# Depthwise convolution of a Conformer block: four channel tiles on each of two engines, and shifted copies placed by DMAs

## The chip, the cores and the metric

The kernel runs on one core of a Trainium2 chip, all in float32. The time is the device time of one execution in microseconds, the median over several runs. Of each kernel one more execution was recorded by the hardware profiler.

The core has engines with instruction streams of their own, which wait for each other by semaphores: TensorE (PE: matmuls and transposes into PSUM, which is used here as a ring of six banks of 512 columns and two fixed ones), VectorE (DVE), ScalarE (ACT), GpSimd (POOL) and SyncE (SP). SyncE issues nearly all DMAs here. Two hardware queues carry DMAs: q1 those of SyncE, q10 those of ScalarE; both are worked off by the same 16 DMA engines.

## The reference, cut to what matters

The program is a Conformer block followed by two attention/convolution layers with mixtures of experts. The change lies in the Conformer's convolution module, near the start. 512 tokens, 1024 channels, eight segments of 64 tokens:

```python
u = h @ w_pw1 + b_pw1                       # 1024 -> 2048
a, gate = jnp.split(u, 2, axis=-1)
u = a * jax.nn.sigmoid(gate)                # GLU
u = dwconv(u.reshape(B * n_seg, L // n_seg, D), w_dw).reshape(B, L, D) + b_dw   # 31 taps, each channel by itself
u = jax.nn.silu(layer_norm(u, ln_g, ln_b))
return u @ w_pw2 + b_pw2
```

The depthwise convolution is zero-padded within each segment: out[t] = sum over k of w[k] * u[t + k - 15].

## The kernel before

Channels lie on partitions, 128 to a tile, so there are eight channel tiles j = 0..7 of 128 x 512. For each tile:

- `pw1(j)` on TensorE: 16 matmuls (32 instructions in the profile) into two banks, one for the gate and one for the value. ScalarE evicts both (L925) into `glu_s` and `glu_a`, which have two buffers each, so `pw1(j)` on ScalarE waits until tile j-2 has been read.
- A tile of `PE_CONV` (0, 2, 4, 6, 7) is convolved on TensorE. The taps are grouped as 31 = 8 rounds of 4 shifts. `urep` (two buffers) holds for each group c of 32 channels the gated tile four times, on partitions 32r to 32r+31 shifted by r tokens; one matmul with a 128 x 32 weight tile then adds four taps for 32 channels, and 32 matmuls (64 instructions, L1540) make the tile. `glu(j)` on VectorE multiplies value and gate in 8 pieces of 32 x 512 straight into the places of r = 0 and 1 (L2309). `spread` on ScalarE copies to the places of r = 2 and 3 in 8 pieces (L933). GpSimd makes the tap weights `taps` (two buffers, L759). `conv_out` evicts with the bias (L940).
- A tile of `DVE_CONV` (1, 3, 5) is convolved on VectorE by `own_conv(j)`: the GLU into a padded buffer (L2316), then 31 multiply-adds of 128 x 512, each waiting for the one before (L2324, L2328).

`conv_mean(j)` (L1550) adds each finished tile to a mean over channels in a fixed bank; after the last one, `mean_done` lets ScalarE, then VectorE go on with the layer norm. `mod_gemv(1)` (L1489) is a matrix-vector product for later modulation parameters; `mod_turn(1)` (L1506) transposes its row.

The order on each engine is written out by hand. On TensorE `mod_gemv(1)` stands between conv(6) and conv(7). Two mean sums, conv(7), `mod_turn(1)` and the last two mean sums follow.

SyncE issues the weight loads in the order of a list, each as soon as the earlier owner of its slot in a six-slot ring is done (L531 to L541). The loads that matter here: one adaptation block of 2 MB (rows of 8 KB) each when pw1(1), pw1(3), pw1(5) and pw1(7) have ended; then two more such blocks and the two 2 MB blocks of w_pw2 (rows of 2 KB), all four released by the end of `mod_gemv(1)` (`mod_row` = 2). Behind the load for pw1(5) SyncE issues eight small loads (L646 to L650).

Of the kernel before, what the change touches and what calls it, by code (L numbers as in the profile page):

```python
# [12 lines left out]
P = 128  # L13
# [24 lines left out]
N_TAPS = 12  # L38
PE_CONV = (0, 2, 4, 6, 7)
DVE_CONV = (1, 3, 5)  # L40
# [19 lines left out]
for _n, _w in (  # L60
    ("c", 8), ("c2", 8), ("cctx", 8), ("norm1_g", 8), ("norm2_g", 8), ("final_g", 8), ("b_pw1", 16), ("b_dw", 8),
    ("ln_g", 8), ("ln_b", 8), ("b_pw2", 8), ("mix_g", 16), ("ffn_g", 16),
    ("b_mod0", 48), ("b_mod1", 48), ("w_conv3", 24), ("q_g", 1), ("k_g", 1), ("subln", 1), ("to_next_row", 5),
    ("b_mod2", 48), ("w_own0", TAPS), ("w_own1", TAPS), ("to_next_block", 18),
    ("w_dw", ROUNDS * 32), ("w_own2", TAPS),
):
    COL[_n] = _at
    _at += _w
VEC_ROWS = [128, 123, 48 + 2 * TAPS, 128, 128, TAPS]
# [47 lines left out]
def block_kernel(nc, A, out):  # L117
# [31 lines left out]
    for j in range(DT):  # L149
        T_PW1[j] = tiles(["act"] * 2)  # L150
        if j == 0:
            T_TAPS = tiles(["dve"])
        if j % 2:
# [102 lines left out]
    with ExitStack() as ctx:  # L256
# [18 lines left out]
        vecT = sb("vecT", [P, 5 * P + TAPS])  # L275
# [75 lines left out]
        glu_s = carve(arena, 11264, 2, N)  # L351
        hid = carve(arena, 0, 16, N)
# [70 lines left out]
        for name in (  # L423
# [6 lines left out]
            "u_base", "u_ready", "u_spread", "u_own", "conv_done", "mean_done", "mean_sb", "centered",  # L430
            "x_pw2", "gains", "hid_ready", "mlp_wsum", "mlp_wsum4", "mlp_tsum", "mlp_part", "mlp_m1", "mlp_read",
            "x_mlp", "rope_tab", "f_folded", "feature_w", "x_sq", "x_sq_used", "x_ms", "x_ms_sb", "x_rms", "x_inv", "x_wide", "x_scaled", "c_ms", "c_rms", "c_inv", "ctx_scaled", "ctx_ready", "lam_sum", "lam_exp",
            "in_hsum", "in_wsum", "in_part", "in_m1", "in_read", "qk_raw", "qk_sq", "qk_ms", "qk_root", "qk_inv", "qk_scaled", "qk_turn", "qk_roped", "qk_turned", "qk_done",
            "scores", "score_half", "neg_max", "probs", "attn_ready", "attn_turned", "aT_sb", "pv_done", "o_in", "o_eps", "o_ms",
            "o_rms", "o_inv", "o_scaled", "o_turned", "o_ready",
            "router_gain", "affine_in", "router_shift", "logit_parts", "logit_parts_sb", "shift_sb", "logits_ready", "soft_exp", "aff_ready", "pos_ready", "left_ready", "left_turned", "chosen",
# [93 lines left out]
        def _(sp):  # L530
# [100 lines left out]
            def load_taps():  # L631
# [6 lines left out]
                for m, j in enumerate(DVE_CONV):  # L638
                    dst = vec_rows[0:TAPS, 5, :] if m == 2 else vec_rows[48 + TAPS * m:48 + TAPS * (m + 1), 2, :]
# [44 lines left out]
        def _(pool):  # L684
# [67 lines left out]
            for m, j in enumerate(PE_CONV):  # L752
                if m >= 2:
                    pool.wait_ge(S["tile_done"], T_CV[PE_CONV[m - 2]] + 1)
                elif m == 0:
                    pool.wait_ge(*emptied(T_TAPS)(0))
# [64 lines left out]
        def _(act):  # L821
# [511 lines left out]
        def _(pe):  # L1333
# [197 lines left out]
            def conv(j):  # L1531
# [4 lines left out]
                pe.wait_ge(S["u_ready"], m + 1)  # L1536
                pe.wait_ge(S["u_spread"], m + 1)
# [7 lines left out]
            def conv_mean(j):  # L1545
# [664 lines left out]
        def _(dve):  # L2210
# [85 lines left out]
            def glu(j):  # L2296

                m = PE_CONV.index(j)
                u = urep[m % 2]
                dve.wait_ge(*emptied(T_PW1[j])(1))  # L2300
                if m >= 2:
                    dve.wait_ge(S["tile_done"], T_CV[PE_CONV[m - 2]] + 1)
                elif m == 0:
                    dve.wait_ge(S["pads_zero"], 5)
                for r in (0, 1):
                    for c in range(SHIFTS):
                        a, s = (x[32 * c:32 * c + 32, j % 2, :].rearrange("p (s w) -> p s w", s=SEGS)
                                for x in (glu_a, glu_s))
                        ins = dve.tensor_tensor(u[32 * r:32 * r + 32, c, :, PAD - r:PAD - r + SEG], a, s, ALU.mult)  # L2309
                    ins.then_inc(S["u_ready" if r else "u_base"], 1)  # L2310

            def own_conv(j):

                m = DVE_CONV.index(j)
                dve.wait_ge(*emptied(T_PW1[j])(1))
# [4 lines left out]
                for k in range(TAPS):  # L2320
# [6 lines left out]
                    else:  # L2327
                        ins = dve.scalar_tensor_tensor(out=acc, in0=u, scalar=w, in1=acc, op0=ALU.mult, op1=ALU.add)  # L2328
# [738 lines left out]
```

## Time and profile before

| | us |
|---|---|
| median of 3 runs | 2239.44 (2238.3 to 2242.77) |
| profiled execution | 2237.22 |
| its span | 2235.4 |
| PE busy | 2165.0 (97%) |
| DVE busy | 967.1 (43%) |
| ACT busy | 396.1 (18%) |
| POOL busy | 73.0 (3%) |

The profile covers the span from the first to the last instruction. Its page gives for each engine busy time and share; the chain that ended last is 83% PE, 11% DMA, 3% DVE and 1% ACT. TensorE's clock was granted at 0.987 of full speed on the mean. The Conformer's convolution stage lies between about 37 and 198 us. Answers of the trace for single stretches (timelines, packets per DMA queue, windows) are used besides the page; all their times count from the span's start.

### The profile page before, as it was taken

The page shows a single profiled execution, that of the slowest core. Times are in us where ns is not written, and L with a number is a line of the kernel's source. Part 1 is how long each engine was busy: PE and PEld are TensorE (multiplying, and loading weights), DVE is VectorE, ACT ScalarE, POOL GpSimd, SP SyncE. Part 2 cuts the span into 40 slices and gives each one's busy share as a digit, 9 for nine tenths or more (in the row PEclk, how much of TensorE's full clock was granted, in tenths as well). Part 3 has the DMA queues.
Part 4 walks back from the last instruction along what each step waited for, and adds up shares of the span by engine and source line. Part 5 has one row for each costly group of instructions (what it writes and reads, how often), then busy time and mean ns, then how long its engine had stood idle before and what let it go on. Part 6 is the DMA issues. An engine that isn't in the chain of part 4 may idle for free.

```text
span 2235.4 us, 24839 instructions
## 1 busy us (share of the span) xinstructions
PE 2165.0 (97%) x10126; PEld 1289.8 (58%) x10126; DVE 967.1 (43%) x1403; ACT 396.1 (18%) x781; POOL 73.0 (3%) x92
## 2 busy tenths in 40 slices
PE   7999999999999999998999999999999899999998
PEld 3343488888886777855444444437884544444443
DVE  3883297787855544833112222215551322222222
ACT  3214222002113122842100000002000200000000
POOL 1100100000012000000000000001001000000000
PEclk9999999999999999998999999999999899999999
DMA  9316234567650112032899999997111599999996
GB/s 353 155 44 234 105 137 164 205 247 271 219 207 22 54 45 83 1 151 113 355 429 429 428 429 428 428 414 264 38 76 75 228 425 428 428 429 429 428 429 269
DMA packets 106459, 564.23 MB, mean 252 GB/s; under 512 B 8840, under 2 KB 17550, under 8 KB 78734
## 3 DMA queue, kind: packets, MB, share of 16 engines
q1 hardware_dynamic: 105952, 563.03, 62.6%
q8 instruction: 54, 0.88, 0.2%
q14 instruction: 23, 0.19, 0.0%
q10 hardware_dynamic: 430, 0.13, 0.0%
HBM read 561.04 MB, written 2.10 MB: 252 GB/s over the span
## 4 chain that ended last, share of the span: by engine, by line
PE 83%; DMA 11%; DVE 3%; ACT 1%; issue 1%; DVEq 0%; SPq 0%; POOL 0%; ACTq 0%
PE psum L1593 20%; PE psum L2036 16%; PE psum L1347 10%; PE psum L2022 8%; DMA ring<-in_moe_w_down_dram 6%; PE psum L2115 5%; PE psum L1741 4%; PE psum L2072 3%; PE psum L1765 3%; PE psum L1922 2%; DMA ring<-in_mlp_w_dram 2%; PE psum L1898 2%; PE psum L1873 2%; DMA ring<-in_moe_w_up_dram 2%; PE psum L1540 2%; PE psum L1489 1%
## 5 line engine op out<-in xcount | busy, mean ns | idle before, releaser
L2036 PE MATMUL psum<-ring,arena 128*64 128x512 f32 x2048 | 444.6, 593 | 5.1 <-DMA ring<-in_moe_w_up_dram 5.1
L2036 PEld LDWEIGHTS psum<-ring,arena 128*64 128x64 f32 x2048 | 145.0, 137 | 301.4 <-issue 287.0
L2022 PE MATMUL psum<-ring,arena 128*64 128x512 f32 x768 | 224.5, 594 | 2.1 <-DMA ring<-in_moe_w_down_dram 2.1
L2884 DVE TENSOR_TENSOR arena<-psum,arena 128x512 f32<-128x512 f32 x32 | 33.9, 1059 | 410.1 <-PE psum L2036 410.1
L1347 PE MATMUL psum<-hT,ring 128*128 128x512 f32 x416 | 180.6, 593 | 3.0 <-ACT hT L888 3.0
L1593 PE MATMUL psum<-ring 128*128 128x256 f32 x640 | 142.9, 380 | 3.8 <-DVE rstd L2467 3.8
L1593 PE MATMUL psum<-hT,ring 128*128 128x256 f32 x608 | 138.9, 385 | 0.8 <-ACT hT L882 0.8
L1347 PEld LDWEIGHTS psum<-hT,ring 128*128 128x128 f32 x416 | 78.6, 190 | 101.6 <-issue 96.9
L1593 PEld LDWEIGHTS psum<-ring 128*128 128x128 f32 x640 | 121.0, 190 | 23.6 <-issue 7.5
L2072 PEld LDWEIGHTS psum<-arena 128*128 128x128 f32 x1024 | 119.7, 196 | 14.0 <-issue 14.0
L1593 PEld LDWEIGHTS psum<-hT,ring 128*128 128x128 f32 x608 | 117.1, 193 | 18.4 <-issue 2.2
L2072 PE MATMUL psum<-arena 128*128 128x128 f32 x1024 | 123.9, 281 | 2.5 <-DVE arena L2911 2.5
L2022 PEld LDWEIGHTS psum<-ring,arena 128*64 128x64 f32 x768 | 73.5, 137 | 73.5 <-issue 73.5
L2022 PE MATMUL psum<-hT,arena 128*64 128x512 f32 x256 | 113.2, 595 | 1.7 <-issue 1.7
L2115 PE MATMUL psum<-arena 128*128 128x512 f32 x256 | 114.1, 599 | 0.0
L2903 DVE SCALAR_TENSOR_TENSOR xT<-psum,modv,xT 128x512 f32<-128x512 f32 x128 | 96.1, 751 | 17.8 <-PE psum L2115 5.8
L1593 PE MATMUL psum<-arena,ring 128*128 128x256 f32 x448 | 99.8, 380 | 3.0 <-DMA ring<-in_mlp_w_dram 3.0
L2898 DVE COPY arena<-psum 128x512 f32<-128x512 f32 x16 | 11.1, 692 | 204.7 <-PE psum L2022 204.7
L1593 PEld LDWEIGHTS psum<-arena,ring 128*128 128x128 f32 x448 | 84.4, 190 | 17.8 <-DMA ring<-in_mlp_w_dram 4.2
L2115 PEld LDWEIGHTS psum<-arena 128*128 128x128 f32 x256 | 47.3, 190 | 66.6 <-issue 66.6
L1275 ACT ACTIVATE arena<-psum 128x512 f32<-128x512 f32 x32 | 19.1, 597 | 327.7 <-PE psum L2036 327.7
L2328 DVE SCALAR_TENSOR_TENSOR arena<-arena,vecT 128x512 f32<-128x512 f32 x90 | 72.3, 803 | 3.2
(384 smaller groups left out, 2555.9 us busy)
## 6 DMA issues: line engine op xcount, KB each, us to landing
ring<-in_moe_w_gate_dram SPq DMA_DIRECT2D x64, 2048.0 KB, 19.2
ring<-in_moe_w_up_dram SPq DMA_DIRECT2D x64, 2048.0 KB, 16.2
ring<-in_moe_w_down_dram SPq DMA_DIRECT2D x44, 2048.0 KB, 19.8
ring<-in_ada_w_dram SPq DMA_DIRECT2D x24, 2048.0 KB, 8.6
ring<-in_mlp_w_dram SPq DMA_DIRECT2D x16, 2048.0 KB, 8.6
hT<-in_moe_w_down_dram SPq DMA_DIRECT2D x16, 2048.0 KB, 14.5
ring<-in_w_mod_dram SPq DMA_DIRECT2D x12, 2048.0 KB, 12.7
ring<-in_conv_w_in_dram SPq DMA_DIRECT2D x6, 2048.0 KB, 19.4
```

The source lines that it names most:

```text
L1347: ins = pe.matmul(bank[:, 0:width], w[:, k, col:col + P], src(k), start=start and k == 0, stop=stop and k == kts - 1)
L1540: ins = pe.matmul(bank[32 * c:32 * c + 32, :, :], taps[m % 2][:, g, c, :], u[:, c, :, SHIFTS * g:SHIFTS * g + SEG], start=g == 0, stop=g = ...
L1593: ins = pe.matmul(psum[:, t % 6, H * i:H * i + H], w[:, k, P * i:P * i + P], src[:, k, :], start=first and i == 0 and k == 0, stop=True, s ...
L1741: ins = pe.matmul(psum[:, t % 6, at:at + width], src[:, k, :], w[:, k, :], start=first and k == 0, stop=k == DT - 1, skip_group_check=True)
L1765: ins = pe.matmul(psum[:, t % 6, H * i:H * i + H], hs[:, k, P * i:P * i + P], ws[:, k, :], start=first and i == 0 and k == 0, stop=True, s ...
L1873: ins = pe.matmul(psum[:, banks + bank, at:at + hi - lo], qT[64 * c:64 * c + 64, h, m * P:(m + 1) * P], kT[64 * c:64 * c + 64, h, lo:hi], ...
L2022: ins = pe.matmul(psum[64 * e:64 * e + 64, bank + nh, :], src[:, 4 * h + k, 64 * e:64 * e + 64], w[:, k, nh * N:(nh + 1) * N], start=h == ...
L2036: ins = pe.matmul(psum[64 * nh:64 * nh + 64, bank + e, :], src[:, 4 * h + k, 64 * e:64 * e + 64], w[:, k, nh * N:(nh + 1) * N], start=h == ...
L2072: ins = pe.matmul(psum[:, 6 + half, (fj % 4) * P:(fj % 4 + 1) * P], h_tok[:, tt, fj * P:(fj + 1) * P], hot[:, tt, :, :].rearrange("p a b - ...
L2115: pe.matmul(psum[:, SCATTER[fj % 3], :], y_sb[:, fj * P:(fj + 1) * P], gselT, start=True, stop=True)\
L2328: ins = dve.scalar_tensor_tensor(out=acc, in0=u, scalar=w, in1=acc, op0=ALU.mult, op1=ALU.add)
L2903: dve.scalar_tensor_tensor(out=xT[:, fj, :], in0=psum[:, SCATTER[fj % 3], :], scalar=modv[:, 1 + 2 * layer, 40 + fj:41 + fj], in1=xT[:, fj ...
```

## The change

TensorE now convolves tiles 2, 4, 6, 7, and VectorE 0, 1, 3, 5. VectorE's own tiles need one more set of tap weights, hence one more small load by SyncE and a second transposed tile of taps. `glu(j)` for a TensorE tile is one multiplication of 128 x 512 into `rms` or `rstd`, buffers that are free in this stage. `spread(m)` on ScalarE no longer copies: it issues 16 DMAs, one for each r and c, each moving 32 partitions x 8 segments of 64 numbers (256 B) from there into `urep`. TensorE waits for their semaphore, `u_spread0` or `u_spread1`. The order on TensorE, ScalarE and VectorE is new.

```diff
@@ -35,9 +35,10 @@
 H = N // 2
 EPS = 1e-6
 N_VEC = 21
-N_TAPS = 12
-PE_CONV = (0, 2, 4, 6, 7)
-DVE_CONV = (1, 3, 5)
+N_TAPS = 13
+PE_CONV = (2, 4, 6, 7)
+DVE_CONV = (0, 1, 3, 5)
+MEANS = (0, 2, 1, 4, 3, 6, 5, 7)
 UPAD = SEG + TAPS - 1
 LAM_INIT = 0.2
 RING = 6
...
@@ -349,6 +350,7 @@
         upad = carve(arena, 2 * UREP + (DT - 1) * N, SEGS, UPAD)
         glu_a = carve(arena, 10240, 2, N)
         glu_s = carve(arena, 11264, 2, N)
+        glu_out = [rms[:, :], rstd[:, :]]
...
@@ -926,13 +929,16 @@
                                    bias=vecT[:, col:col + 1]).then_inc(FREE["act"], 1)
 
             def spread(m):
+
                 u = urep[m % 2]
-                act.wait_ge(S["u_base"], m + 1)
-                for r in (2, 3):
+                act.wait_ge(S["u_ready"], m + 1)
+                if m >= 2:
+                    act.wait_ge(S["tile_done"], T_CV[PE_CONV[m - 2]] + 1)
+                for r in range(SHIFTS):
                     for c in range(SHIFTS):
-                        ins = act.activation(u[32 * r:32 * r + 32, c, :, PAD - r:PAD - r + SEG],
-                                             u[0:32, c, :, PAD:PAD + SEG], ACT.Copy)
-                ins.then_inc(S["u_spread"], 1)
+                        act.dma_start(u[32 * r:32 * r + 32, c, :, PAD - r:PAD - r + SEG],
+                                      glu_out[m % 2][32 * c:32 * c + 32, :].rearrange("p (s w) -> p s w", s=SEGS))\
+                            .then_inc(S[f"u_spread{m % 2}"], 16)
 
             def conv_out(j):
                 t = T_CV[j]
@@ -940,14 +946,16 @@
                 act.activation(cv[:, j, :], psum[:, t % 6, :], ACT.Identity,
                                bias=vecT[:, COL["b_dw"] + j:COL["b_dw"] + j + 1]).then_inc(FREE["act"], 1)
 
-            for m in range(4):
-                pw1(2 * m)
+            pw1(0)
+            pw1(1)
+            for m in range(3):
+                pw1(2 * m + 2)
                 spread(m)
-                pw1(2 * m + 1)
-                conv_out(2 * m)
-                if m == 3:
-                    spread(4)
-            mod_row(1)
+                pw1(2 * m + 3)
+                if m == 2:
+                    spread(3)
+                    mod_row(1)
+                conv_out(2 * m + 2)
             act.wait_ge(S["conv_done"], len(DVE_CONV))
             conv_out(DT - 1)
             mod_turned(1)
...
@@ -1533,8 +1541,7 @@
                 u = urep[m % 2]
                 bank = begin(t).rearrange("p (s w) -> p s w", s=SEGS)
                 pe.wait_ge(S["taps_ready"], m + 1)
-                pe.wait_ge(S["u_ready"], m + 1)
-                pe.wait_ge(S["u_spread"], m + 1)
+                pe.wait_ge(S[f"u_spread{m % 2}"], 16 * SHIFTS * SHIFTS * (m // 2 + 1))
...
-                return pe.matmul(psum[:, STAT, :], const("ones_d"), cv[:, j, :], start=j == 0, stop=j == DT - 1)
-
-            for m in range(4):
-                pw1(2 * m)
-                if m == 0:
-                    pe.wait_ge(S["taps_in"], 16 * N_TAPS)
-                    pe.wait_ge(S["tap_pad"], 1)
-                    turn_tile(T_TAPS, [(vec_rows[0:VEC_ROWS[g], g, :], VEC_ROWS[g]) for g in range(2, 6)])
-                if m == 2:
-                    pe.wait_ge(S["rms_ready"], 1)
-                if m >= 2:
-                    conv_mean(2 * m - 3)
-                pw1(2 * m + 1)
-                conv(2 * m)
-                if m == 3:
-                    mod_gemv(1)
-                if m:
-                    conv_mean(2 * m - 2)
-            conv_mean(5)
+                return pe.matmul(psum[:, STAT, :], const("ones_d"), cv[:, j, :], start=j == MEANS[0], stop=j == MEANS[-1])
+
+            pw1(0)
+            pe.wait_ge(S["taps_in"], 16 * N_TAPS)
+            pe.wait_ge(S["tap_pad"], 1)
+            for m in range(2):
+                turn_tile(T_TAPS + m, [(vec_rows[0:VEC_ROWS[g], g, :], VEC_ROWS[g]) for g in (2 + 2 * m, 3 + 2 * m)])
+            pw1(1)
+            pw1(2)
+            pw1(3)
+            conv(2)
+            pw1(4)
+            pe.wait_ge(S["rms_ready"], 1)
+            conv_mean(0)
+            conv_mean(2)
+            pw1(5)
+            conv(4)
+            pw1(6)
+            conv_mean(1)
+            conv_mean(4)
+            pw1(7)
+            conv_mean(3)
+            mod_gemv(1)
+            conv(6)
             conv(7)
             mod_turn(1)
             conv_mean(6)
+            conv_mean(5)
             conv_mean(7).then_inc(S["mean_done"], 1)
...
@@ -2296,22 +2309,16 @@
             def glu(j):
 
                 m = PE_CONV.index(j)
-                u = urep[m % 2]
                 dve.wait_ge(*emptied(T_PW1[j])(1))
                 if m >= 2:
-                    dve.wait_ge(S["tile_done"], T_CV[PE_CONV[m - 2]] + 1)
-                elif m == 0:
-                    dve.wait_ge(S["pads_zero"], 5)
-                for r in (0, 1):
-                    for c in range(SHIFTS):
-                        a, s = (x[32 * c:32 * c + 32, j % 2, :].rearrange("p (s w) -> p s w", s=SEGS)
-                                for x in (glu_a, glu_s))
-                        ins = dve.tensor_tensor(u[32 * r:32 * r + 32, c, :, PAD - r:PAD - r + SEG], a, s, ALU.mult)
-                    ins.then_inc(S["u_ready" if r else "u_base"], 1)
-
-            def own_conv(j):
+                    dve.wait_ge(S[f"u_spread{m % 2}"], 16 * SHIFTS * SHIFTS * (m // 2))
+                dve.tensor_tensor(glu_out[m % 2], glu_a[:, j % 2, :], glu_s[:, j % 2, :], ALU.mult).then_inc(S["u_ready"], 1)
+
+            def own_conv(j, between=None):
 
                 m = DVE_CONV.index(j)
+                if m:
...
+                        if between is not None and k == TAPS // 2:
+                            glu(between)
...
-            for j in range(DT):
-                if j in PE_CONV:
-                    glu(j)
-                else:
-                    own_conv(j)
+            dve.wait_ge(S["pads_zero"], 5)
+            own_conv(0)
+            glu(2)
+            own_conv(1)
+            glu(4)
+            own_conv(3)
+            own_conv(5, 6)
+            glu(7)
```

TensorE around its last two convolutions. Before: L1540 is a convolution (`tmp` or `sq` hold the tap weights), L1489 `mod_gemv(1)`, L1550 a mean sum.

```order
L1540 MATMUL psum<-arena,tmp 32x512 [waits u_ready,u_spread,taps_ready,act_free]
L1540 MATMUL psum<-arena,tmp 32x512 x31
L1489 MATMUL psum<-ring,cpad 32x512 [waits landed2,mod_raw_ready]
L1489 MATMUL psum<-ring,cpad 32x512 x7
...
L1550 MATMUL psum<-arena,K 128x512 [waits act_free]
L1550 MATMUL psum<-arena,K 128x512 [waits conv_done]
L1540 MATMUL psum<-arena,sq 32x512 [waits u_ready,u_spread,taps_ready,act_free]
L1540 MATMUL psum<-arena,sq 32x512 x31
L1506 MATMUL psum<-K,mod_rows 128x128 [waits mod_row_sb]
```

The same place now; L1547 is a convolution, L1497 `mod_gemv(1)`, L1557 a mean sum.

```order
L1557 MATMUL psum<-arena,K 128x512 [waits conv_done]
L1497 MATMUL psum<-ring,cpad 32x512 [waits landed2,mod_raw_ready]
L1497 MATMUL psum<-ring,cpad 32x512 x7
...
L1547 MATMUL psum<-arena,sq 32x512 [waits u_spread0,taps_ready,act_free]
L1547 MATMUL psum<-arena,sq 32x512 x31
L1547 MATMUL psum<-arena,tmp 32x512 [waits u_spread1,taps_ready,act_free]
L1547 MATMUL psum<-arena,tmp 32x512 x31
L1514 MATMUL psum<-K,mod_rows 128x128 [waits mod_row_sb]
```

`mod_gemv(1)` has moved ahead of conv(6), and conv(7) follows conv(6) at once.

VectorE at the end of the stage, before: a GLU in eight pieces (L2309), the last own convolution (L2316 to L2328, tile 5), and the GLUs of tiles 6 and 7.

```order
L2309 TENSOR_TENSOR arena<-arena 32x8x64 [waits tile_done,act_free]
L2309 TENSOR_TENSOR arena<-arena 32x8x64 x7
L2316 TENSOR_TENSOR arena<-arena 128x8x64 [waits act_free]
L2324 TENSOR_SCALAR arena<-arena,vecT 128x512 [waits dve_link]
L2328 SCALAR_TENSOR_TENSOR arena<-arena,vecT 128x512 [waits u_own]
L2328 SCALAR_TENSOR_TENSOR arena<-arena,vecT 128x512 [waits dve_link] x29
L2309 TENSOR_TENSOR arena<-arena 32x8x64 [waits tile_done,act_free]
L2309 TENSOR_TENSOR arena<-arena 32x8x64 x7
L2309 TENSOR_TENSOR arena<-arena 32x8x64 [waits tile_done,act_free]
L2309 TENSOR_TENSOR arena<-arena 32x8x64 x7
```

The same now: tile 5 (L2323 to L2337) with the GLU of tile 6 (L2315, into `rms`) in its middle, and the GLU of tile 7 behind it.

```order
L2323 TENSOR_TENSOR arena<-arena 128x8x64 [waits act_free,conv_done]
L2331 TENSOR_SCALAR arena<-arena,vecT 128x512 [waits dve_link]
L2337 SCALAR_TENSOR_TENSOR arena<-arena,vecT 128x512 [waits u_own]
L2337 SCALAR_TENSOR_TENSOR arena<-arena,vecT 128x512 [waits dve_link] x13
L2315 TENSOR_TENSOR rms<-arena 128x512 [waits u_spread0,act_free,dve_link]
L2337 SCALAR_TENSOR_TENSOR arena<-arena,vecT 128x512
L2337 SCALAR_TENSOR_TENSOR arena<-arena,vecT 128x512 [waits dve_link] x15
L2315 TENSOR_TENSOR rstd<-arena 128x512 [waits u_spread1,act_free]
```

The eight-piece GLUs have become single instructions, and that of tile 6 stands after 14 of the 30 multiply-adds of tile 5.

ScalarE's new spreads, with the evictions of pw1 (L928) and the convolutions (L946) about the last two.

```order
L939 DMA arena<-rms 32x8x64 [waits tile_done,u_ready]
L939 DMA arena<-rms 32x8x64 x15
L928 ACTIVATE arena<-psum,vecT 128x512 [waits u_own,tile_done] x2
L939 DMA arena<-rstd 32x8x64 [waits tile_done,u_ready]
L939 DMA arena<-rstd 32x8x64 x15
L895 ACTIVATE mod_rows<-psum 128x512 [waits mod_row]
L946 ACTIVATE arena<-psum,vecT 128x512 [waits tile_done]
L946 ACTIVATE arena<-psum,vecT 128x512 [waits tile_done,conv_done]
```

Sixteen DMA issues stand where eight copies stood; the row of `mod_gemv(1)` (L895) is now evicted behind the last spread.

## Rows read from the trace of the kernel before

**Rows 1.** Chain that ended last: start us, us, what; 37 to 374 us.
```profile
37.33 13.97 PE psum L1347 x32
...
65.72 7.00 PE psum L1540 x64
...
100.39 7.00 PE psum L1540 x64
...
173.16 7.00 PE psum L1540 x64
180.16 6.87 PE psum L1489 x64
...
195.95 0.59 PE psum L1506 x4
196.53 1.73 PE psum L1550 x4
...
373.06 8.32 DMA ring<-in_mlp_w_dram
```

**Rows 2.** Timeline of DVE, 45 to 200 us: start, us, line, operation, idle before.
```profile
53.51 8.56 DVE L2309 TENSOR_TENSOR arena<-arena 32x512 f32<-32x512 f32 x8
...
66.48 0.69 DVE L2316 TENSOR_TENSOR arena<-arena 128x512 f32<-128x512 f32 x1 [4.40 <-ACT arena L925]
...
92.82 5.56 DVE L2309 TENSOR_TENSOR arena<-arena 32x512 f32<-32x512 f32 x8
...
198.92 1.29 DVE L2350 TENSOR_TENSOR arena<-arena,tmp 128x512 f32<-128x512 f32 x2 [19.43 <-ACT tmp L956]
```

**Rows 3.** Timeline of ACT, 0 to 60 us; ACTq are its DMA issues.
```profile
3.97 0.33 ACTq L525 DMA_DIRECT2D arena<-in_conv_ln_b_dram  x1
...
6.33 0.48 ACTq L525 DMA_DIRECT2D arena<-in_b_mod_dram  x1
...
51.34 0.69 ACT L925 ACTIVATE arena<-psum,vecT 128x512 f32<-128x512 f32 x1 [6.18 <-PE psum L1347]
```

**Rows 4.** Timeline of SP, 50 to 420 us: DMA issues.
```profile
137.21 0.47 SPq L646 DMA_DIRECT2D lam_in<-in_lam_q_dram  x1
...
141.30 2.27 SPq L650 DMA_DIRECT2D rw<-in_router_w_dram  x2
...
173.19 14.78 SPq L541 DMA_DIRECT2D ring<-in_w_mod_dram  x3
```

**Rows 5.** DMA packets in 100.3 to 101.3, 101.8 to 107.2, 203 to 207 us.
```profile
DMA packets 0, 0.00 MB, mean 0 GB/s; under 512 B 0, under 2 KB 0, under 8 KB 0
...
DMA packets 250, 1.99 MB, mean 369 GB/s; under 512 B 7, under 2 KB 7, under 8 KB 7
...
DMA packets 772, 1.55 MB, mean 387 GB/s; under 512 B 16, under 2 KB 16, under 8 KB 772
```

**Rows 6.** DMA packets by queue in 36 to 37 and in 143 to 152 us.
```profile
DMA packets 937, 0.17 MB, mean 167 GB/s; under 512 B 907, under 2 KB 923, under 8 KB 937
...
q1 hardware_dynamic: 937, 0.17, 92.3%
...
q1 hardware_dynamic: 2990, 0.57, 31.8%
```

**Rows 7.** DMA packets by queue in 11 to 12 us; q10 is ACT's.
```profile
DMA packets 94, 0.40 MB, mean 403 GB/s; under 512 B 12, under 2 KB 47, under 8 KB 47
...
q1 hardware_dynamic: 47, 0.39, 97.0%
q10 hardware_dynamic: 47, 0.02, 7.7%
```

**Rows 8.** Windows: us, engines' busy time, PEclk, DMA share, GB/s.
```profile
277.00:281.00 4.00, 3.79 (x9) 3.10 (x10) 3.77 (x8) 3.26 (x9) 0.00 (x0) 0.50 0.19 69
281.00:285.00 4.00, 4.00 (x19) 3.50 (x19) 4.00 (x10) 3.38 (x8) 0.00 (x0) 0.99 0.00 0
198.00:200.40 2.40, 0.25 (x1) 0.01 (x1) 1.48 (x3) 1.35 (x3) 0.00 (x0) 1.00 0.99 388
```

More of the change, by code:

```diff
@@ L64 @@
     ("b_mod2", 48), ("w_own0", TAPS), ("w_own1", TAPS), ("to_next_block", 18),
-    ("w_dw", ROUNDS * 32), ("w_own2", TAPS),
+    ("w_dw", ROUNDS * 32), ("w_own2", TAPS), ("w_own3", TAPS),
 ):
@@ L68 @@
     _at += _w
-VEC_ROWS = [128, 123, 48 + 2 * TAPS, 128, 128, TAPS]
+VEC_ROWS = [128, 123, 48 + 2 * TAPS, 128, 128, 2 * TAPS]
 KCOL = {}
@@ L151, in block_kernel @@
         if j == 0:
-            T_TAPS = tiles(["dve"])
-        if j % 2:
+            T_TAPS = tiles(["dve"] * 2)
+        if j % 2 and j > 1:
             T_CV[j - 1] = tiles(["act"])
@@ L274, in block_kernel @@
         K = sb("K", [P, KW])
-        vecT = sb("vecT", [P, 5 * P + TAPS])
+        vecT = sb("vecT", [P, 5 * P + 2 * TAPS])
         cpad = sb("cpad", [P, DT, 32])
@@ L429, in block_kernel @@
             "n_ms", "n_inv", "n_wide", "half_scaled", "half_ready", "late_sq",
[L430 removed]
+            "u_ready", "u_spread0", "u_spread1", "u_own", "conv_done", "mean_done", "mean_sb", "centered",
             "x_pw2", "gains", "hid_ready", "mlp_wsum", "mlp_wsum4", "mlp_tsum", "mlp_part", "mlp_m1", "mlp_read",
[L432 to L433 removed]
+            "x_mlp", "rope_tab", "f_folded", "feature_w", "x_sq", "x_sq_used", "x_ms", "x_ms_sb", "x_rms", "x_inv", "x_wide", "x_scaled", "c_ms", "c_rms", "c_inv", "ctx_scaled", "lam_sum", "lam_exp",
+            "in_hsum", "in_wsum", "in_part", "in_m1", "in_read", "qk_raw", "qk_sq", "qk_ms", "qk_root", "qk_inv", "qk_roped", "qk_turned", "qk_done",
             "scores", "score_half", "neg_max", "probs", "attn_ready", "attn_turned", "aT_sb", "pv_done", "o_in", "o_eps", "o_ms",
             "o_rms", "o_inv", "o_scaled", "o_turned", "o_ready",
[L436 removed]
+            "router_gain", "affine_in", "router_shift", "logit_parts", "logit_parts_sb", "shift_sb", "logits_ready", "soft_exp", "aff_ready", "left_ready", "left_turned", "chosen",
             "hot_ready", "gsel_ready", "gathered", "xs_act", "xs_dve", "gselT_done", "gselT_sb",
@@ L638, in load_taps @@
                 for m, j in enumerate(DVE_CONV):
-                    dst = vec_rows[0:TAPS, 5, :] if m == 2 else vec_rows[48 + TAPS * m:48 + TAPS * (m + 1), 2, :]
+                    at, g = (48 + TAPS * m, 2) if m < 2 else (TAPS * (m - 2), 5)
+                    dst = vec_rows[at:at + TAPS, g, :]
                     rows(sp, dst, A["conv_w_dw"][0][:, j * P:(j + 1) * P], "taps_in")
@@ L755, in _ @@
                 elif m == 0:
-                    pool.wait_ge(*emptied(T_TAPS)(0))
+                    pool.wait_ge(*emptied(T_TAPS)(1))
                     pool.wait_ge(S["sq_used"], DT)
@@ L2331, in own_conv @@
                 ins.then_inc(S["conv_done"], 1)
-            dve.wait_ge(S["tile_done"], T_TAPS + 1)
             for g in range(2, 6):
-                w = VEC_ROWS[g]
-                ins = dve.tensor_copy(vecT[:, g * P:g * P + w], psum[:, T_TAPS % 6, (g - 2) * P:(g - 2) * P + w])
-                if g < 5:
+                w, t = VEC_ROWS[g], T_TAPS + g // 2 - 1
+                dve.wait_ge(S["tile_done"], t + 1)
+                ins = dve.tensor_copy(vecT[:, g * P:g * P + w], psum[:, t % 6, g % 2 * P:g % 2 * P + w])
+                if g % 2:
+                    ins.then_inc(FREE["dve"], 1)
+                else:
                     link(ins)
-            ins.then_inc(FREE["dve"], 1)
-            dve.wait_ge(*emptied(T_TAPS)(0))
+            dve.wait_ge(*emptied(T_TAPS)(1))
             link(dve.memset(upad[:, :, 0:PAD], 0.0))
             link(dve.memset(upad[:, :, PAD + SEG:UPAD], 0.0))
-            for j in range(DT):
-                if j in PE_CONV:
-                    glu(j)
-                else:
-                    own_conv(j)
+            dve.wait_ge(S["pads_zero"], 5)
[6 more added lines that the diff above has]
+            glu(7)
             dve.wait_ge(S["mean_sb"], 1)
```

1 line of the change is left out of this document (added).

## The prediction

> **What bounds the kernel now.** I read the chain of waits first. From 37.33 us to 196.53 + 1.73 = 198.3 us it holds nothing but TensorE: eight first pointwise layers pw1 (L1347, 13.7 to 14.0 us for 32 matmul instructions), five convolutions (L1540, 7.00 us each), the mean sums (L1550), the adaptation product mod_gemv(1) (L1489, 6.87 us) and small transposes [rows 1]. So in this stage TensorE's own work is the time: a convolution taken from it is worth up to 7.00 us, and anything that makes it wait costs its full length. VectorE's timeline comes second. It ends its last GLU near 179 us and then stands idle for 19.43 us until the means are there [rows 2], so it has room for one more convolution. Third comes the traffic: which transfers SyncE's queue issues at what time [rows 4], and how the 16 DMA engines share themselves between two queues [rows 5 to 7].
>
> **What leaves TensorE.** conv(0) goes: −7.00 us [rows 1]. The four tap transposes become two tiles of two with the same work, and the eight means stay eight. From the same rows I shift the points that matter. pw1(3) ends at 100.39 − 7.00 = 93.4. pw1(7) ends at 173.16 − 7.00 = 166.2. mod_gemv(1) now stands ahead of conv(6), with five means before it for four: it ends at 180.16 + 6.87 − 14.00 + 0.87 = 173.9. conv(6) and conv(7) would then run from 173.9 to 187.9, and with mod_turn (0.59) and three means (3 × 0.87) the stage would end at 191.2 for 198.3 before: −7.1 us, if TensorE never waits.
>
> **What VectorE gets.** One own convolution lasts from 66.48 to 92.82, 26.34 us [rows 2]. The GLU for a TensorE tile falls from eight pieces (5.56 us) to one whole multiplication, for which I take the 0.69 us of L2316. Its dates: own_conv(0) starts where glu(0) did, 53.5 to 79.9. glu(2) needs pw1(2), done at 79.5 and evicted in 0.69 [rows 3]: ready at 81.0. own_conv(1) 81.0 to 107.4. glu(4) waits for pw1(4), done at 93.4 + 7.00 + 13.7 = 114.1: VectorE stands 7 us, and the GLU is ready at 115.6. own_conv(3) to 142.0. own_conv(5) with glu(6) in its middle (ready at 155.7) to 169.1. glu(7) ready at 169.9. The last sum is not late for its mean; what matters is that glu(7) is ready at 169.9 and conv(7) wants its data at 180.9.
>
> **What the placing costs.** ScalarE loses eight copies per tile (4.44 us) and issues 16 DMAs of 32 partitions × 8 pieces of 256 B: 4096 packets, 256 for each of the 16 engines. No row shows a DMA from SBUF to SBUF. Issue: ScalarE's take 0.33 to 0.48 us, SyncE's 128-packet ones 0.47, the 1024-packet ones 1.13 on average [rows 3, 4]. I take 0.47, by the nearest in packets, so 16 × 0.47 = 7.5 us; the ends are 0.33 (5.3 us) and 1.13 (18 us). Movement with nothing beside it: 937 mostly short packets moved in 1 us at 92.3% busy, 15.8 ns of one engine for each [rows 6], so 256 take 4.0 us and hide behind the issue. From issue to first packet a big load takes over 1 us (the one released by pw1(3)'s end at 100.3 has no packet to 101.3 and flows from 101.8) [rows 1, 5]; I use 1.3 for both queues and let 2 us stand for issue to semaphore.
> With that the first three are covered: spread(0) 81.0 + 7.5 + 2 = 90.5 for a need at 93.4; spread(1) 125.1 for 129.7 (pw1(5)'s end); spread(2) 165.2 for 173.9. While ScalarE issues, pw1's evictions wait up to 7.5 us; TensorE has six banks and doesn't notice.
>
> **The fourth meets the weight loads.** SyncE is held by mod_gemv(1): when it ends, SyncE issues the two remaining adaptation blocks and the two pw2 blocks, 8 MB in a row. Before, that was at 180.16 + 6.87 = 187.03, and the spreads were no transfers; now it is at 173.9 [rows 1, 4]. spread(3) issues from 169.9 to 177.4. By 173.9 it has 4.0 / 0.47 = 8.5 of its 16 DMAs out; the load of slot 1 (issued at 166.2, packets to about 173.0) has left the engines just before, and by 175.2, when the 8 MB arrive, these 8.5 are moved. 7.5 DMAs remain: 120 packets per engine.
> How do two queues share an engine? Between 11 and 12 us ScalarE's queue (q10) had short rows waiting beside adaptation loads on q1: 47 packets of the one went through and 47 of the other, and the engines were full [rows 7]. These were loads with three rows and a semaphore write per engine (35 rows and 12 under 512 B), so each short packet waited for one 8 KB packet, not each DMA. In the Trainium skill, DMA: Bandwidth & Descriptors, section Queues, rings and completion order, the engine goes round robin between its queues, packet by packet; by that rule, the trace agrees (47 to 47), but its further statement is a rival below.
> A pair takes 16 / 47 = 0.34 us on one engine. The two adaptation blocks are 256 packets each [rows 5], together 32 per engine: 32 × 0.34 = 10.9 us. The pw2 blocks come in 2 KB packets, 772 in 4 us or 0.083 us each [rows 5]; with a short one 0.099: the other 88 take 8.7 us. So spread(3) has landed at 175.2 + 19.6 + 0.2 = 195.0, and conv(7), wanted at 180.9, waits 14.1 us. Nothing stands before it on TensorE that could be done meanwhile: mod_turn and the last means are queued behind it.
> Then the clock. After the wide gap near 271 to 276 us the granted clock stood at 0.50 (1.2 GHz) from 277 to 281, with 9 matmuls where the next 4 us at 0.99 held 19: ten times 0.21 us, 2.1 us lost. After the 2.4 us gap at 198 it stayed 1.00 [rows 8]. A wait of 14 us is of the first kind: +2.1 us (bounds 0 and 7.0, all of conv(7) at 1.2 GHz).
> Sum: −7.1 + 14.1 + 2.1 = +9.1 us. Behind the stage TensorE's work and the loads that it releases follow each other (a load at 373.06 begins as TensorE gives its slot back [rows 1]), so I carry the shift to the end unchanged. Profiled execution: 2237.22 + 9.1 = 2246.3. The median of the runs shown lies 2.2 above it: 2248.5 us.
>
> **Rivals.**
> *Everything lands in time (20%).* If several of the short packets pass in one turn, spread(3) keeps ahead of conv(7). From nine on: 120 / 9 = 13 turns of 0.32 and 120 × 0.0158 us, 6.1 us, so 181.3, a wait of 0.4; from ten on, none. Then −7.1 us stands: 2232.4. For it: the rows that met the loads were loads from HBM with at most four packets per engine and DMA, these have 17. Against it: the even count, which held even with four. The Trainium skill, same page and section, has this as a rule: a whole packet of typically 9 to 17 descriptors is drained before the engine switches; by it the time would be about 2232. The count of rows 7 shows single ones.
> *Issue is quick, the meeting short (10%).* At 0.33 us per issue, 12 of 16 DMAs are out by 173.9, and 64 packets per engine remain: 32 × 0.34 + 32 × 0.099 = 14.1 us, landed at 189.4, a wait of 8.5. −7.1 + 8.5 + 2.1 = +3.5: 2243, not to be told from no change.
> *Every spread is slow (10%).* The six 128-packet loads and two of 1024 issued from 137 us on moved 2990 packets in the 9 us from 143 us on at 31.8% busy, up to 1.1 us per DMA [rows 4, 6]: if a small DMA costs this, or issue costs 1.13, a spread takes about 16 to 18 us and 2 to land. spread(0) lands near 99, and its end falls into the load issued at 93.4, so 101: a wait of 7.6. spread(1) lands some 4 to 7 us late, spread(3) at about 198. With three fallen clocks: −7.1 + 7.6 + 5.5 + 17 + 5 = +28: 2267. Against it: at 36 us seven such DMAs' worth of packets passed in 1 us [rows 6].
>
> **How the numbers follow.** The forecast has 60%; its own range, from the bounds of issue (0.40 to 0.6 us) and clock (0 to 4 us), is 2243 to 2254. The 80% range must hold the hidden case too and leaves most of the slow-spread one out: 2231 to 2259. A measurement tells 0.2%, about 4.5 us, from no change. Faster is the hidden case and little else: 0.21. Within 0.2%: the short meeting and the low end of the forecast, 0.10. Slower: 0.69.
>
> **What the profile of the changed kernel would show.** Right: one wait of TensorE of 12 to 16 us ahead of the last convolution, ended by a DMA; packets of q10 and q1 in equal number from about 175 us; clock near 0.5 behind it; no wait ahead of the first three convolutions; VectorE idle 7 us ahead of glu(4). Wrong: conv(7) following conv(6) at once; q10 packets many times those of q1; issues of 1 us on ScalarE; or a later stage that gives the shift back.

## The result

The changed kernel is slower: 2256.74 us median of 5 runs (2252.23 to 2259.08) for 2241.83 of the kernel before in the same measurement (5 runs, 2238.3 to 2242.77). The ratio is 1.0066, 95% interval 1.0053 to 1.0079. A second measurement gave 2257.95 for 2241.8, ratio 1.0071 (1.0054 to 1.0087). The forecast was 2248.5, +9.1 us; it is +14.9 and +16.2. That lies inside the 80% range (2231 to 2259) and above the range that the forecast gave for itself (2243 to 2254).

The profiled execution took 2254.87 us (span 2253.1), 17.65 more than the one before. The chain that ended last, through the stage of the change; it answers to [rows 1]. Columns: start us, us, what.

```profile
37.64 16.54 PE psum L1355 x32
...
94.39 2.17 DMA arena<-rms
...
96.70 7.07 PE psum L1547 x64
...
178.47 1.72 ACTq L939
...
182.22 3.77 ACTq L939
...
186.01 16.73 DMA arena<-rstd
...
202.88 8.92 PE psum L1547 x64
211.80 0.59 PE psum L1514 x4
212.39 2.59 PE psum L1557 x6
```

The place to read is 186.01: the last of the DMAs that place tile 7 is issued there and lands 16.73 us later; conv(7) starts at 202.88, and its 64 instructions take 8.92 us for 7.00. In the waits of TensorE between 37 and 300 us (total, times, longest) the two of the convolutions are

```profile
PE psum L1547 <- DMA arena<-rstd: 18.6, 1, 18.6
...
PE psum L1547 <- DMA arena<-rms: 0.6, 1, 0.6
```

conv(7) waits 18.6 us, conv(2) 0.6, conv(4) and conv(6) not at all. ScalarE's timeline has the spreads, 16 DMA issues each:

```profile
84.38 10.65 ACTq L939 DMA_DIRECT2D arena<-rms  x16
...
158.57 10.52 ACTq L939 DMA_DIRECT2D arena<-rms  x16
...
171.65 18.29 ACTq L939 DMA_DIRECT2D arena<-rstd  x16
```

An undisturbed spread is issued in 10.5 to 10.65 us, about 0.63 us and a gap of 0.03 for each DMA, and the last DMA lands 2.2 us after its own issue began. The fourth took 18.29 us to issue: three single issues, at 178.47, 182.22 and 186.01 us, took 1.72, 3.77 and 3.93 us. VectorE and SyncE's queue, answering to [rows 2] and [rows 4]:

```profile
118.46 0.69 DVE L2315 TENSOR_TENSOR rstd<-arena 128x512 f32<-128x512 f32 x1 [7.78 <-ACT arena L928]
...
170.93 0.68 DVE L2315 TENSOR_TENSOR rstd<-arena 128x512 f32<-128x512 f32 x1
```

```profile
169.57 9.00 SPq L543 DMA_DIRECT2D ring<-in_w_mod_dram  x3
178.61 10.60 SPq L543 DMA_DIRECT2D ring<-in_conv_w_pw_dram  x2
```

VectorE stands 7.78 us ahead of glu(4), and glu(7) starts at 170.93. SyncE issues the block released by pw1(7) at 169.57, the next two when mod_gemv(1) has ended at 177.2, and the pw2 blocks from 178.61. Packets per queue (packets, MB, share of 16 engines) in 178 to 180, 188 to 190 and 196 to 198 us, answering to [rows 7]:

```profile
q10 hardware_dynamic: 1042, 0.25, 116.3%
q1 hardware_dynamic: 14, 0.11, 27.7%
...
q1 hardware_dynamic: 96, 0.79, 98.1%
q10 hardware_dynamic: 96, 0.02, 5.5%
...
q1 hardware_dynamic: 299, 0.59, 89.6%
q10 hardware_dynamic: 302, 0.07, 17.6%
```

From 178 to 180 the spread has the engines nearly alone. Later each queue moves one packet for one of the other: 96 beside 96 of 8 KB, 302 beside 299 of 2 KB. From 180 us to the end q10 moved 1959 packets, 122 for each engine (semaphore writes counted).

There are two stretches in which the queues don't take turns. From 172 to 175 us the block released by pw1(7) flows; the spread, issued from 171.65 on, moves nothing at all, so q10 has no row. From 180 to 183 us the 8 MB have just begun:

```profile
q1 hardware_dynamic: 153, 1.25, 100.4%
...
q1 hardware_dynamic: 131, 1.07, 93.9%
q10 hardware_dynamic: 64, 0.02, 4.3%
```

The queue wasn't empty: by 180.2 us 11 DMAs of 17 packets per engine were issued, 2992 packets, and up to 180 us 2393 had moved, so about 37 per engine were waiting. In both stretches a load that has begun shortly before flows on q1 while packets issued on q10 wait. No run shows why.

The clock (PEclk is the third last column), answering to [rows 8]:

```profile
38.00:42.00 4.00, 4.00 (x5) 1.46 (x5) 3.31 (x6) 4.00 (x7) 0.00 (x0) 0.50 0.79 247
...
190.00:202.80 12.80, 0.00 (x0) 0.00 (x0) 0.00 (x0) 1.16 (x2) 0.00 (x0) 0.50 1.06 342
...
202.80:206.00 3.20, 3.12 (x16) 0.90 (x20) 0.00 (x0) 0.00 (x0) 0.00 (x0) 0.50 0.44 161
...
206.00:212.00 6.00, 6.00 (x54) 1.84 (x47) 0.00 (x0) 0.08 (x1) 0.00 (x0) 0.95 0.00 0
```

PEclk fell to 0.50 (1.2 GHz) in the long wait and stayed there to about 206 us. It also stood at 0.50 from 38 to 42 us, in the first pw1, which took 16.54 us for 13.97.

So the 17.65 us are: 0.3 us by which the stage began later; 2.6 in the first pw1 (clock); −7.0 for conv(0); 0.6 ahead of conv(2); 18.6 ahead of conv(7); 1.9 in conv(7) (clock). That makes 17.0, in a stage whose end moved by 16.7; the 0.3 between them were not traced. mean_done came at 214.98 for 196.53 + 1.73 = 198.26 in the kernel before [rows 1], and the shift stayed to the end.

### The profile page after: what moved, and what is told of

It is laid out like the page before. It is cut to its first block, busy times and chain, and to the rows that moved or that the text cites. A ratio compares the mean times of both kernels' runs of the same rounds, so it can differ in the third digit from the quotient of the medians.

```text
span 2253.1 us, 24730 instructions
## 1 busy us (share of the span) xinstructions
PE 2165.2 (96%) x10062; PEld 1292.8 (57%) x10062; DVE 964.7 (43%) x1399; ACT 373.3 (17%) x740; POOL 70.7 (3%) x91
## 4 chain that ended last, share of the span: by engine, by line
PE 62%; issue 23%; DMA 7%; DVE 6%; ACTq 1%; ACT 1%; POOL 0%; DVEq 0%; SPq 0%; POOLq 0%
PE psum L1606 21%; PE psum L2049 8%; PE psum L1355 7%; PE psum L2035 4%; PE psum L1754 4%; PE psum L1778 3%; DMA ring<-in_moe_w_down_dram 3%; DVE arena L2337 3%; PE psum L2128 3%; PE psum L1935 2%; PE psum L2085 2%; PE psum L1911 2%; PE psum L1886 2%; DMA ring<-in_mlp_w_dram 1%; ACTq L939 1%
## 5 line engine op out<-in xcount | busy, mean ns | idle before, releaser
L2337 DVE SCALAR_TENSOR_TENSOR arena<-arena,vecT 128x512 f32<-128x512 f32 x120 | 93.3, 777 | 4.2
## 6 DMA issues: line engine op xcount, KB each, us to landing
ring<-in_moe_w_up_dram SPq DMA_DIRECT2D x64, 2048.0 KB, 16.2
ring<-in_w_mod_dram SPq DMA_DIRECT2D x12, 2048.0 KB, 13.7
```

## The experiments

My theory after this, called the turns theory: conv(7)'s wait is the meeting of the spread of tile 7 with 8 MB of weight loads, and its length comes from packets taking turns. The rivals: the DMAs are slow by themselves; the spread comes behind all of the loads; the loss is elsewhere. "Before" in the times of the first four is 2243.75 us, the median of 14 runs (2239.05 to 2247.38).

**Loads held until the spread has landed (e1_hold).**

```diff
                 if prev_of[n] is not None:
...
+                if n == B_MOD[2][2]:
+                    sp.wait_ge(S["u_spread1"], 2 * 16 * SHIFTS * SHIFTS)
```

> The changed kernel, but SyncE issues the two adaptation blocks and the two pw2 blocks (8 MB) only when the spread of tile 7 has landed. Turns theory (the 18.6 us wait ahead of conv(7) comes from sharing the 16 DMA engines packet by packet with these loads): spread(3) takes 10.5 us of issue and 2.2 to land, as spread(0) did, so about 183.5 us in the trace of the changed kernel, and conv(7) waits 0 to 2 us for 18.6; no fallen clock there; the whole is 17 to 20 us faster than the changed kernel, about 2237 to 2240. The loads end near 206 us and are wanted at about 200 (first half) and 210, so they cost nothing. Rival (the DMAs are slow by themselves: sixteen issues behind a busy ScalarE): conv(7) still waits over 8 us. Rival (most of the loss is elsewhere, such as the 2.6 us at the stage's start): the gain stays under 10 us.

Measured: 2233.28 us (2232.0 to 2235.82, 5 runs), ratio to before 0.9954 (0.9941 to 0.9968). TensorE's wait for tile 7, and ScalarE's issue of it:

```profile
PE psum L1549 <- DMA arena<-rstd: 1.3, 1, 1.3
```

```profile
171.88 12.22 ACTq L941 DMA_DIRECT2D arena<-rstd  x16
```

One wait in SyncE's program takes 23.5 us from the changed kernel's time. TensorE's wait is 1.3 us for 18.6, and the last spread is issued in 12.22 us for 18.29. So the issues of 3.77 and 3.93 us belong to the meeting. That of 1.72 us doesn't: with the loads held, one issue still takes 1.59 us at the same place, 179.19. The rivals "slow by themselves" and "elsewhere" fall. The time lies below the 2237 to 2240 expected, of which more below.

**mod_gemv(1) back between the two convolutions (e2_between).**

```diff
-            mod_gemv(1)
             conv(6)
+            mod_gemv(1)
             conv(7)
```

> The changed kernel with mod_gemv(1) between conv(6) and conv(7), as before the change: same work, other order, and the 8 MB are released 7 us later. Turns theory: spread(3) has left the engines when they come; conv(6), wanted at about 170.5, now waits some 1 to 3 us for spread(2), conv(7) not at all or under 2 us; 15 to 19 us faster than the changed kernel, about 2238 to 2242. Rival (slow by themselves): the wait only moves to conv(6) and conv(7), over 8 us in sum.

Measured: 2233.03 us (2230.94 to 2235.78, 4 runs), ratio 0.9953 (0.9938 to 0.9969). The waits of the convolutions:

```profile
PE psum L1547 <- DMA arena<-rms: 1.0, 2, 0.6
...
PE psum L1547 <- DMA arena<-rstd: 0.2, 1, 0.2
```

With the same work in another order conv(7) waits 0.2 us. The waits for the other buffer are 0.6 us ahead of conv(2) and 0.4 ahead of conv(6), less than the 1 to 3 expected, and the time lies below the 2238 to 2242 expected. What costs isn't the transfers by themselves but the loads released beside them.

**The same bytes in smaller packets (e3_two_kb).**

```diff
...
+                elif n in B_MOD[2][2:]:
+                    for q in range(4):
+                        sp.dma_start(slot_like(slot, src)[:, :, q * N:(q + 1) * N], src[:, :, q * N:(q + 1) * N])\
+                            .then_inc(landed[slot], 16)
```

> The changed kernel, but each of the two adaptation blocks that meet the spread is loaded by four DMAs of a quarter of the columns: the same bytes in packets of 2 KB for 8 KB. Turns theory (one packet of each queue in turn): a turn of the spread costs 0.1 us for 0.34, so the packets left, some 100 to 115 per engine, take about 11 us for 18 to 20; conv(7)'s wait falls from 18.6 to 9 to 12 us, though all bytes are the same. Rival (the engines share by bytes, or the spread simply comes behind the loads): the wait stays at 17 to 20 us. In time 7 to 10 us faster than the changed kernel, or no change.

Measured: 2249.34 us (2247.53 to 2251.19, 9 runs), ratio to before 1.0026 (1.0016 to 1.0036), 7.4 us faster than the changed kernel's first median. TensorE's wait, and the queues from 188 to 190 us:

```profile
PE psum L1551 <- DMA arena<-rstd: 13.7, 1, 13.7
```

```profile
q1 hardware_dynamic: 302, 0.58, 89.4%
q10 hardware_dynamic: 304, 0.07, 18.0%
```

The wait fell by 4.9 us to 13.7, and 9 to 12 was expected, so that number missed; the rival, no change, is ruled out. The 7.4 us in time lie within the 7 to 10 expected, but the stage's end came only 4.3 us earlier (210.6 for 215.0), so part of them isn't the wait and stays unexplained. The counts say why the wait was longer than expected: from 180 us on the spread had 2210 packets left, 138 per engine, where I had taken 100 to 115. At 302 to 304 packets in 2 us a turn takes 0.105 us, and 138 turns 14.5 us; the spread landed at 197.66, about 17.7 us after 180, with a slow stretch from 182 to 184 (63 packets, beside 345 of q1) like that of the changed kernel. What decides is the number of turns left and what stands in each.

**Copies on ScalarE for the DMAs (e4_copies).**

```diff
-                        act.dma_start(u[32 * r:32 * r + 32, c, :, PAD - r:PAD - r + SEG],
-                                      glu_out[m % 2][32 * c:32 * c + 32, :].rearrange("p (s w) -> p s w", s=SEGS))\
-                            .then_inc(S[f"u_spread{m % 2}"], 16)
+                        ins = act.activation(u[32 * r:32 * r + 32, c, :, PAD - r:PAD - r + SEG],
+                                             glu_out[m % 2][32 * c:32 * c + 32, :].rearrange("p (s w) -> p s w", s=SEGS),
+                                             ACT.Copy)
+                ins.then_inc(S[f"u_spread{m % 2}"], 1)
...
```

> The changed kernel with the DMAs of spread replaced by sixteen copies of 32 x 512 on ScalarE, from the same gated tile to the same places: 16 x 0.555 = 8.9 us by the copies of the kernel before. It tells what the split of tiles (four and four) brings without the transfers. Theory: the split is worth its 7 us when the placing is hidden: spread(3) is ready about 180.5 in the changed kernel's trace, before conv(7) wants it; no wait of TensorE for ScalarE above 1 us; about 7 us faster than the kernel before, 2232 to 2237. Rival (ScalarE is blocked 8.9 us per tile and evicts pw1 late, or VectorE with four own convolutions is the bound): waits of TensorE for evictions or means of several us, and no gain over the kernel before.

Measured: 2232.6 us (2228.55 to 2234.3, 5 runs), ratio 0.9953 (0.9939 to 0.9966): faster than both kernels. ScalarE's last spread:

```profile
169.68 10.30 ACT L939 ACTIVATE arena<-rstd 32x512 f32<-32x512 f32 x16 [1.40 <-DVE rstd L2316]
```

From one copy to the next it was 0.64 us, not 0.555, so a spread takes 10.3 us; it is ready at 180.0, and conv(7) starts at 182.1, when conv(6) is done. None of the convolutions waits. The split of four and four is sound; ScalarE places a tile itself in no more time than it needs to issue the DMAs for it.

**Half the segments (e5_half_seg).** Each DMA places segments 0 to 3 only, so half of the shifted copies is missing.

```diff
-                        act.dma_start(u[32 * r:32 * r + 32, c, :, PAD - r:PAD - r + SEG],
+                        act.dma_start(u[32 * r:32 * r + 32, c, 0:SEGS // 2, PAD - r:PAD - r + SEG],
...
```

> The changed kernel, but each DMA of spread places only the first four of eight segments (128 packets for 256; the other half of the shifted copies is left out). An issue took 0.63 us on ScalarE where I had 0.47. If an issue costs by its packets, it falls to about 0.45 us and a spread to 7.5 us; if it costs by the DMA, it stays at 0.6 us and the spread at 10.5 us. Turns theory: when the 8 MB come at about 180, half of the 122 packets per engine are left, 61: 30 of them beside 8 KB packets, 31 beside 2 KB, 10.2 + 3.3 us, so conv(7) waits 9 to 12 us for 18.6. Rival (the spread comes behind the loads whatever its size): the wait stays above 16 us.

Measured: 2244.2 us in one run, before 2241.8 (7 runs). Wait, an undisturbed spread's issue, and the queues from 184 to 186 us:

```profile
PE psum L1548 <- DMA arena<-rstd: 10.6, 1, 10.6
```

```profile
155.54 10.39 ACTq L939 DMA_DIRECT2D arena<-rms  x16
```

```profile
q1 hardware_dynamic: 96, 0.79, 98.6%
q10 hardware_dynamic: 96, 0.02, 5.6%
```

128 packets are issued in the 0.65 us of 256: the issue costs by the DMA. The wait is 10.6 us, within the 9 to 12 that the turns gave, and the queues are even again. A spread that came behind all of the loads would have waited over 16. For a time it does come behind them, though: from 177 to 179 us, with 18 packets per engine or more issued and not moved, q10 has no row in the view, and q1 is alone:

```profile
q1 hardware_dynamic: 101, 0.83, 102.6%
```

And from 175.93 us on, beside these loads, no issue takes over 0.72 us, so loads on the other queue are not enough to make an issue slow.

**Where does the clock at the stage's start come from? (e6_before_again, e7_after_again: both kernels unchanged.)**

> The kernel before once more, for a second profile. Its profiled execution (2237.2 us) was the shortest of all its runs (median 2243.8 of 14). If the missing 3 to 6 us are the clock at the start of the stage, the first pw1 takes about 16.5 us here for 13.97, with the granted clock near 0.5 from 38 to 42 us, as in the profiles of the changed kernel and of the first four experiments; then the gain of 10 to 11 us in the timed runs of the hidden versions is not larger than their 7 us by the change. If the first pw1 takes 14 us again, the kernel before loses its time elsewhere.

> The changed kernel once more. Turns theory: again a wait of 17 to 20 us ahead of conv(7) and about 2 us of half clock behind it; 13 to 17 us slower than the kernel before on this chip. If the wait differs by several us from run to run, the meeting with the loads depends on chance.

The kernel before took 2241.79 us in this execution. Its first pw1, and its window from 38 to 42 us:

```profile
36.77 15.70 PE psum L1347 x32
```

```profile
38.00:42.00 4.00, 4.00 (x7) 1.59 (x6) 2.12 (x4) 3.98 (x6) 0.00 (x0) 0.69 0.89 274
```

15.70 us for 13.97, with the clock at 0.69: the slow first pw1 is the kernel before's too, and its first profile was a lucky one. The changed kernel again took 2257.95 us (2256.21 to 2259.45, 4 runs), with

```profile
PE psum L1547 <- DMA arena<-rstd: 20.5, 1, 20.5
```

```profile
203.51 9.29 PE psum L1547 x64
```

20.5 us of wait for 18.6, just over the 17 to 20 expected, and 9.29 us of conv(7): the meeting is there both times, and its size moves by 2 us. Single issues took 4.43 and 4.18 us here.

**More profiles (e8_before_c, e9_before_d: the kernel before; e10_copies_again; e11_hold_again).** The held and copied versions gained 10 to 11 us, more than conv(0)'s 7.

> The kernel before, third profile. The versions with the spread hidden are 10 to 11 us faster in the timed runs, but their stage (start to mean_done) is only 3.4 (held loads) to 7.1 us (copies) shorter than in the kernel before's second profile. Theory A: the feed-forward part behind the stage (from the first L1593 to the first L1741 matmul: 416.6 and 418.3 us in the two profiles before, 414.1 to 417.3 in seven of the changed kind) is longer in the kernel before by some 2 us, and more in its slower runs. Then this profile shows 417 or more there. Theory B: it is scatter of the clock anywhere; then this part lies within 415 to 417 and the missing microseconds appear at another place or not at all.

> The kernel before, fourth profile; expectation as for the third. If its whole time is above 2243, the stretch that is long against the first profile (2237.2 us) tells where the slower runs lose.

> The copies version, second profile. Theory A: 414 to 416 us from the first L1607 to the first L1755 matmul (the same two places); the stage ends at 191 to 194 us. Theory B: that part can be 417 or more here too.

> The held-loads version, second profile. Turns theory: conv(7) waits 1 to 2 us again and the stage ends at 194 to 197 us. Theory A: about 415 us in the feed-forward part; theory B: anywhere in 414 to 418.

From each profile I took the start of the token sums behind pw2 (L1374 in the kernel before) and the length of the feed-forward part as the expectation defines it. All in us; "run" is the time of the profiled execution.

| kernel | run | token sums start | feed-forward part |
|---|---|---|---|
| before | 2237.2, 2241.8, 2241.4, 2243.1 | 270.1, 271.2, 274.9, 273.0 | 416.6, 418.3, 415.3, 417.2 |
| changed | 2254.9, about 2256.2 | 286.8, 289.5 | 417.3, 416.0 |
| held loads | 2235.1, 2233.6 | 267.9, 266.6 | 415.3, 414.7 |
| copies | 2228.6, 2231.6 | 264.1, 264.2 | 414.1, 415.4 |
| mod_gemv(1) between | 2233.0 | 266.6 | 415.8 |

(The second run of the changed kernel is its span, 2254.4, and 1.8.) By the means, the copies version is at the token sums 272.3 − 264.15 = 8.1 us ahead of the kernel before, and gains another 2.1 in the feed-forward part. At the end of the stage itself (the last mean sum) the kernel before is at 198.3, 199.4, 201.4 and 199.7 us and the copies version at 192.3 and 192.4: 7.3 us apart, which is what conv(0) was said to be worth. Both copies and held loads ended the stage where expected (192.4 and 194.8 us in the second profiles), and conv(7) waited 1.3 us again with the loads held. Theory A, "417 or more in each profile before", falls with 415.3; "some 2 us on the mean" stands on four profiles against two and is within their scatter. The first pw1 explains none of it on the mean: it took 13.97 to 16.57 us in the kernel before, 15.5 on the mean, and 15.5 in both profiles of the copies. The step from 7.3 to 8.1 us is the clock behind the stage: from the last mean sum to the token sums it is 72 us in two profiles before and in both of the copies, and 1.5 to 1.7 us more in the third and fourth before, where the clock stood at 0.57 on the mean from 203 to 207 and from 202 to 206 us. What remains of the 3 to 4 us beyond conv(0)'s 7, mostly the 2.1, stays open.

## Why the prediction was right, and where it was off

**TensorE is the bound, conv(0) is worth 7 us:** right. With the placing hidden the stage ends 7.3 us earlier and the run is 11 us shorter (copies), of which some 3 are outside the stage and not explained.

**VectorE's dates:** right. It stood 7.78 us ahead of glu(4) (7 forecast). glu(7) was ready at 171.6, which is 168.7 when the 2.9 us are taken off by which pw1(0) ended later; 169.9 was forecast.

**The first three spreads are hidden:** right but for 0.6 us at conv(2).

**The issue at 0.47 us:** the term that was mis-sized. It took 0.66 with its gap, 10.5 us for 7.5. The nearest row by number of packets was the wrong measure, since the cost doesn't go by packets (e5_half_seg). In the Trainium skill, DMA: Bandwidth & Descriptors, section Issuing engines are not separate DMA queues, the time to issue is said to be usually small relative to the DMA itself. These runs differ: 10.5 us of issue for movement that needs 4.0 us by [rows 6], since the DMAs are small.

**The meeting with the loads:** right in place and cause: the 8 MB released by mod_gemv(1), one packet for one once both flow. The count, 122 packets per engine left where 120 were forecast, is right in part by luck. The loads were in full flow 8.4 us after the spread's first issue where 5.3 were forecast: TensorE was 3.3 us late against 1.8 of the spread, and the loads took longer to come. That alone would have left fewer packets; the slower issue, and the one issue of 1.72 us, made up for it. The forecast also took it that the block released by pw1(7) would be out of the way, with no price for meeting it; in fact the spread moved nothing until it had passed (172 to 175 us, 153 packets of q1 and none of q10). The spread had caught up by 180 us, so this cost little here. By the Trainium skill, same page, section Queues, rings and completion order, the engine takes turns between its queues packet by packet; the trace agrees from 183 us on, 96 to 96, and not in the stretches in which a load has just begun (64 beside 131 from 180 to 183 us). Its typical packet of 9 to 17 descriptors, on which the first rival rested, isn't seen: with 16 data rows per engine and DMA the count was as even as with three.

**Its length:** 18.6 and 20.5 us for 14.1; with the issue this is the term that was too small. Of the 4.5 us, some 1.4 are the later coming of the loads: they are in full flow at 180.0, 2.8 us behind the end of mod_gemv(1), and 1.3 were taken. The other 3.1 are the spread's end, which took 22.7 us from 180.0 for 19.6 forecast. A pair with a 2 KB packet took 2 / 300 of a us times 16, 0.107 us for 0.099; that gives 0.7 us for 88 turns. Between 180 and 190 us q10 moved only 406 packets beside 475, nearly all of the lag in the first 3 us. So 1553 packets, 97 per engine, were left at 190 us, when the 8 KB packets were all but through; by an estimate from these counts 7 turns more than forecast fell beside 2 KB packets, another 0.7 us. The rest, 1.7 us, is mostly the end: from 201 to 202.8 us q10 moved its last 24 packets, so the engines didn't finish together.

**The slow issues:** I had taken the issue as free of what SyncE has under way. Those of 3.77 and 3.93 us came only beside the loads, but in e5_half_seg, with half the packets, none did; what holds them was not found. They are not what makes conv(7) late: from 183 us on the queues moved packet for packet (96 beside 96), so q10 was never short of packets: some 75 to 97 per engine were issued and not moved while these two issues lasted. The issue of 1.72 us has its like, 1.36 to 1.91 us, in every profile with this spread as DMAs, loads held or not. It goes each time with one packet of 16 KB of a third queue, here at 178.26 us for 1.50 us:

```profile
q8 instruction: 1, 0.02, 4.7%
```

The times of the two suggest a cause; no run tests it.

**The clock:** 1.9 and 2.3 us for 2.1. The half clock at the stage's start, which makes the first pw1 1.5 to 3.1 us longer, was in none of my rows, since the one profile I had was free of it. Eleven of the thirteen profiles show it, in either kernel. So it isn't an effect of the change, though it is 2.6 of the 17.65 us between the first two profiles.

**The shift stays to the end:** right. 16.7 us at mean_done, 17.65 at the end of that execution.

**The rivals:** none held. In the hidden case conv(7) would have waited 0.4 us at most; an issue took 0.66 us, neither the 0.33 of the short meeting nor the 1.1 of the slow spreads. The sum of +9.1 was 5.8 and 7.1 us low against the timed runs (+14.9, +16.2), and conv(7)'s wait alone was 4.5 and 6.4 us longer than forecast in the two profiles.

## What to carry to other kernels

A transfer of many short packets pays, for each packet, one packet of whatever the other queue has waiting: count the packets left when the bulk load starts, and price each turn by the size of the other's packet. While a load is just beginning, count on nothing: the short packets stood still for up to 3 us here. Before moving a product that releases loads to an earlier place, look at what else wants the DMA engines then; one semaphore wait ahead of the bulk loads was worth 23 us here. And sixteen of these small DMAs were no cheaper for the engine that issued them (10.5 us) than sixteen copies of 32 x 512 (10.3 us).

## What was not expected of the hardware

- A DMA issue on ScalarE took 0.63 us and 0.03 between two, for 128 packets as for 256.
- Beside a second queue's bulk loads single issues took up to 3.93 us, and 4.43 in the second profile; with half the packets per DMA none did (at most 0.72 us from 175.93 us on).
- Packets that had been issued on one queue stood still while a load on the other began: none beside 153 from 172 to 175 us, 64 beside 131 from 180 to 183.
- Copies of 32 x 512 on ScalarE followed each other at 0.555 us from the shifted buffer and at 0.64 from the GLU's result, though one by itself took 0.62 and 0.63.
- The granted clock at the start of the stage differs from run to run of the same program, and no run shows what decides it: TensorE was busy for 1.0 us of the 4 from 34 to 38 us in the first profiles of both kernels, and then ran at 1.00 in the one and at 0.50 in the other. The kernel before's first pw1 took 13.97, 15.70, 16.57 and 15.67 us in its four profiles.
